# A decoder layer on eight cores: V's first pass on unshifted rows, the second norm by tiles, the residual and the down projection's loads asked for earlier

## The chip, the cores and the metric

One Trainium2 chip, eight cores, one program on all of them. The time is that of the slowest core, in microseconds of device time. Each core has TensorE (PE), VectorE (DVE), ScalarE (ACT), GpSimd (POOL, here only the issuer of the weight loads) and SyncE (SP, the issuer of all other transfers). On-chip memory is one hand-managed region of 128 partitions x 53184 words ("arena"); matmuls write to eight PSUM banks of 512 f32.

## The reference, cut to what matters

One layer, D = 4096, four sequences of 2048 tokens, 16 heads, F = 11008:

```python
mod = silu(c) @ w_ada + b_ada        # shift1, scale1, gate1, shift2, scale2, gate2
h = rms(x, norm1_g) * (1 + scale1) + shift1
u, va, q, k, vb, ga, gb = split(h @ w_in)
y_a = gelu(u) * (W_s @ rms(gelu(va)) + b)       # in chunks of 128 tokens
# per head two softmaxes over keys of 128, causal, with ALiBi
y_b = rms((softmax(q1 k1) - lam * softmax(q2 k2)) @ vb) * (1 - lambda_init)
x = x + gate1 * ((sigmoid(ga) * y_a + sigmoid(gb) * y_b) @ w_out)
h2 = rms(x, norm2_g) * (1 + scale2) + shift2
x = x + gate2 * ((silu(conv(h2 @ up_g)) * conv(h2 @ up_v)) @ w_down)
```

## The kernel before

Two cores share a sequence. The even one (half 0) owns tokens 0 to 1119, the odd one (half 1) the rest; it also computes K and V for its context, tokens 0 to 1023, and 94 tokens of its own first block again. Activations lie transposed, features on partitions. Weights stream as slices of 256 columns (4 MB in f32 in memory, cast to 2 MB on chip) through a ring of three slots, `w_run`. A unit is a slice and the code that consumes it; the slice of unit i is asked for at most two units ahead, once its slot's last reader is done (`w_issue`, L410). The order on each engine is the order in which the program is written out; a small clock (`tick`) only decides where background pieces (`bg_set`) and delayed pieces (`later`) are put into it. DMAs of SP and POOL run in two queues.

Stages, in order:

- **Front** (`mixer`, L585 to L622): 16 units of w_ada for scale1, then 16 for shift1, 64 matmuls of one column each (L340 through `ada_unit`). Beside them the first pass over x: squares on ACT (L492), sums on DVE (L494), and for each tile of tokens a matmul with ones (L498), ln and exp. When the last unit is through, the second pass scales (L506) and shifts (L508) x into h. Half 1 does this for its context; two of four tiles of x stay on chip.
- **Context, half 1 only**: for each head K (norm by L533, L539, L543 to L545, store to kc_s) and V (`cv`, cast at L655, store to vc_s). Its own x is filled in beside it, from rings of eight (`fill`).
- **vA** (L674 on): gelu (L682), squares (L683), store to vA_s, 16 heads.
- **Heads**: K, Q, V, gB, gA, u for each. The attention of the head before runs in the background of K, Q and V: scores L805, exp L811, values L823, and at each block's end a tail of small operations (L834 to L847) that frees the banks of the values.
- The other 64 w_ada units stand between these units, one behind every second in half 1, behind each in half 0; six are held back for the last head's attention.
- **Output projection** (`out_proj`): a block is 32 matmuls (L1019) and a DVE operation with the gate and the residual, which is loaded when the block begins (L1014, L1026); the sum goes to x1_s.
- **Second norm** (`norm2`): one root for each tile (L1067), then all x1 read again, scaled (L1075) and shifted (L1077) into h2.
- **Up projection**: 86 units, convolution on DVE, products kept on chip for the first chunks (19 of 86 in half 1, 15 in half 0), stored to act_s for the others.
- **Down projection** (`down`): when the up projection has ended, w_down pieces of 11 chunks go to a ring of four and act_s is loaded back; for each of 32 output rows 86 chunks are summed.

## Time and profile before

| | |
|---|---|
| time, median of the runs shown | 9345.61 us |
| lowest, highest | 9320.87, 9478.41 us |
| profiled execution | 9307.9 us |
| its span, core 7 (half 1, slowest) | 9306.3 us |
| core 6 (half 0, its neighbour) | 9295.3 us |
| all cores | 9282.5 to 9306.3 us |
| core 7: PE, DVE, ACT busy | 8451.6 (91%), 1803.1 (19%), 1996.5 (21%) us |
| core 7: DMA | 1051.87 MB, 113 GB/s |
| largest group | L340 PE, 41728 matmuls, 6446.9 us |

The page divides the span into 40 slices; on core 7 PE's busy tenths are 1, 1, 6 in the first three, then 9 but for a 6 at the 26th. A matmul's own record overlaps its neighbours; where matmuls follow one another without a gap, the stretch divided by their number is the cost of one. The sizes of the DMA queues count what lands; a weight slice is read as twice that. Even cores run one program and odd cores another, so a change has to be followed on both.

### The profile page before, as it was taken

To read this page: it belongs to the slowest core of one execution; us is meant where nothing else is said; L and a number is where in the kernel's file an instruction comes from. 1 tells how busy PE (TensorE), PEld (TensorE's weight loads), DVE (VectorE), ACT (ScalarE), POOL (GpSimd) and SP (SyncE) were. 2 spreads that over 40 slices of the span, in tenths; PEclk is the share of its full clock that TensorE was granted. 3 is DMA by queue.
4 is the path that set the end of the run, shared out by engine and by line. 5 is a ranking of instruction groups with operands and counts; after the bars stand their busy time and mean duration, and the time that the engine had idled before them with its cause. 6 is when DMAs were issued, how large, how long until landed. Compare 5 with 4: busy or idle time off the path is not lost.

```text
span 9306.3 us, 141632 instructions; the slowest of 8 cores (9282.5 to 9306.3 us)
## 1 busy us (share of the span) xinstructions
PE 8451.6 (91%) x56406; PEld 4878.7 (52%) x56406; DVE 1803.1 (19%) x3402; ACT 1996.5 (21%) x4411; POOL 315.9 (3%) x602
## 2 busy tenths in 40 slices
PE   1169999989999999999999989699999999989999
PEld 1146567865565555555555544344444444444444
DVE  2032220001221112222221121322322222200000
ACT  2042221222333333333333320211111111100000
POOL 0000000000000000000000000000000000001111
PEclk9999999999999999999999989899999999999999
DMA  9977776664545544454433366644444444466666
GB/s 193 174 159 151 154 148 124 123 124 94 107 95 107 109 101 101 100 98 94 81 66 83 69 154 143 163 82 82 93 98 92 91 92 96 86 149 113 113 113 105
DMA packets 298092, 1051.87 MB, mean 113 GB/s; under 512 B 29536, under 2 KB 214624, under 8 KB 253664
## 3 DMA queue, kind: packets, MB, share of 16 engines
q0 software_dynamic: 86112, 807.44, 47.5%
q1 hardware_dynamic: 211328, 235.27, 8.3%
q8 instruction: 466, 7.63, 0.3%
q14 instruction: 186, 1.52, 0.1%
HBM read 1770.85 MB, written 79.14 MB: 199 GB/s over the span
## 4 chain that ended last, share of the span: by engine, by line
PE 71%; DMA 18%; DVE 3%; ACT 3%; issue 2%; another core or an unknown queue 1%; SPq 1%; DVEq 0%; ACTq 0%; POOLq 0%
PE ps L340 54%; PE ps L1204 11%; DMA arena<-x_loc 6%; DMA vA_s<-arena 5%; PE ps L823 4%; DMA arena<-w_ada 2%; PE ps L805 2%; DMA vc_s<-arena 2%; DMA arena<-x_ctx 1%; ACT arena L811 1%; DMA kc_s<-arena 1%; ACT arena L842 1%; DVE arena L837 1%; DVE arena L839 1%
## 5 line engine op out<-in xcount | busy, mean ns | idle before, releaser
L340 PE MATMUL ps<-arena 128*128 128x465 bf16 (+3 forms) x41728 | 6446.9, 308 | 378.9 <-DMA arena<-w_ada 242.2
L340 PEld LDWEIGHTS ps<-arena 128*128 128x128 bf16 x41728 | 3588.0, 98 | 2777.7 <-issue 420.7
L1204 PE MATMUL ps<-arena 128*128 128x464 bf16 x5504 | 1087.1, 360 | 33.1 <-DMA arena<-w_down 17.3
L1204 PEld LDWEIGHTS ps<-arena 128*128 128x128 bf16 x5504 | 533.1, 97 | 587.1 <-issue 45.3
L811 ACT ACTIVATE arena<-ps,arena 128x256 bf16<-128x256 f32 (+1 forms) x1600 | 693.0, 456 | 647.4 <-PE ps L805 638.0
L823 PE MATMUL ps<-arena 128*128 128x257 bf16 (+1 forms) x3200 | 614.4, 276 | 144.4 <-ACT arena L811 92.3
L1129 ACT ACTIVATE arena<-ps 128x465 f32<-128x465 f32 x344 | 192.3, 559 | 1900.5 <-PE ps L340 1900.5
L823 PEld LDWEIGHTS ps<-arena 128*128 128x128 bf16 (+1 forms) x3200 | 258.4, 97 | 406.5 <-issue 292.7
L1019 PE MATMUL ps<-arena 128*128 128x465 bf16 x2048 | 417.9, 368 | 28.4 <-DVE arena L1026 27.6
L805 PE MATMUL ps<-arena 128*128 128x128 bf16 (+1 forms) x3200 | 434.8, 218 | 0.0
L1119 DVE TENSOR_SCALAR arena<-arena 128x928 f32<-128x928 f32 x172 | 131.3, 764 | 1487.7 <-ACT arena L1129 1487.7
L1122 DVE SCALAR_TENSOR_TENSOR arena<-arena 128x928 f32<-128x928 f32 x344 | 407.7, 1185 | 36.3 <-DVE arena L1122 0.5
L916 ACT ACTIVATE arena<-ps 128x465 bf16<-128x465 f32 x192 | 107.5, 560 | 1172.2 <-PE ps L340 1166.4
L805 PEld LDWEIGHTS ps<-arena 128*128 128x128 bf16 x3200 | 296.5, 98 | 82.1 <-issue 31.8
L1019 PEld LDWEIGHTS ps<-arena 128*128 128x128 bf16 x2048 | 202.5, 99 | 243.4 <-issue 48.1
L452 DVE TENSOR_TENSOR arena<-ps,arena 128x2 f32<-128x2 f32 x96 | 15.1, 157 | 1493.6 <-PE ps L340 1493.6
L545 DVE SCALAR_TENSOR_TENSOR arena<-ps,arena 128x512 bf16<-128x512 f32 (+1 forms) x192 | 141.0, 735 | 759.3 <-ACT arena L544 647.5
L1209 DVE SCALAR_TENSOR_TENSOR arena<-ps,arena 128x464 f32<-128x464 f32 x64 | 44.9, 701 | 1070.7 <-PE ps L1204 1070.7
L419 POOL DMA_DIRECT2D arena<-w_in x144 | 76.0, 528 | 4679.7 <-PE ps L340 3818.1
L508 ACT ACTIVATE arena<-arena 128x256 bf16<-128x256 f32 x256 | 114.9, 501 | 407.0 <-DVE arena L506 406.9
L492 ACT ACTIVATE arena<-arena 128x256 f32<-128x256 f32 x256 | 102.4, 413 | 381.5 <-DMA arena<-x_ctx 194.1
L533 ACT ACTIVATE arena<-ps 128x512 bf16<-128x512 f32 (+1 forms) x192 | 111.3, 579 | 297.9 <-PE ps L340 260.3
(74 smaller groups left out, 2303.1 us busy)
## 6 DMA issues: line engine op xcount, KB each, us to landing
arena<-w_in POOLq DMA_DIRECT2D x144, 2048.0 KB, 14.2
arena<-w_ada POOLq DMA_DIRECT2D x96, 2048.0 KB, 24.1
arena<-w_up POOLq DMA_DIRECT2D x86, 2048.0 KB, 13.8
arena<-w_down POOLq DMA_DIRECT2D x224, 352.0 KB, 4.8
arena<-x_loc SPq DMA_DIRECT2D x256, 128.0 KB, 4.1
arena<-w_out POOLq DMA_DIRECT2D x16, 2048.0 KB, 14.1
arena<-x_ctx SPq DMA_DIRECT2D x128, 128.0 KB, 3.8
act_s<-arena SPq DMA_DIRECT2D x67, 232.0 KB, 9.2
```

The lines of the kernel that those rows point to most:

```text
L340: fns = [(lambda e, l=l, rr=rr, i=i: e.matmul(out, lhsT=l, rhs=rr, start=(i == 0), stop=(i == n - 1))) for i, (l, rr) in list(enumerate(pa ...
L508: P.op("act", lambda e: e.activation(out=dst[:, fc, a:a + w], in_=xv, func=AF.Identity, bias=self.modT[:, fc:fc + 1], scale=1.0), reads=[x ...
L533: P.op("act", lambda e: e.activation(out=sqb.v[a][:, 0:w], in_=o, func=AF.Square), reads=[self.Bps[bk]], writes=[sqb.b[a]])
L545: P.op("dve", lambda e: e.scalar_tensor_tensor(out=dst, in0=o, scalar=self.cc(gname), in1=rv, op0=ALU.mult, op1=ALU.mult), reads=[self.Bps ...
L805: P.op("pe", [(lambda e, cm=cm: e.matmul(sv[:, cm * w:(cm + 1) * w], lhsT=KT[:, cm, kb * 128:kb * 128 + m], rhs=QT[:, cm, q0:q0 + w], star ...
L811: P.op("act", lambda e: e.activation(out=pv, in_=sv, func=AF.Exp, bias=self.cc("ali", ai)[0:m, :], scale=128.0 ** -0.5), reads=[self.Bps[s ...
L823: P.op("pe", [(lambda e, cm=cm: e.matmul(self.ps[0:w, (6 + cm) * 512:(6 + cm) * 512 + 257], lhsT=self.pT.v[pt][0:m, cm * w:(cm + 1) * w], ...
L1019: fns = [(lambda e, kc=kc: e.matmul(o, lhsT=wv[:, kc, l * 128:(l + 1) * 128], rhs=self.hy[:, kc, t0:t0 + w], start=(kc == 0), stop=(kc == ...
L1119: P.op("dve", lambda e: e.tensor_scalar(out=dst, in0=src[:, 0:NO], scalar1=cw(0), scalar2=self.cc("convb", ch), op0=ALU.mult, op1=ALU.add) ...
L1122: P.op("dve", lambda e, jj=jj: e.scalar_tensor_tensor(out=dst, in0=src[:, jj:NO + jj], scalar=cw(jj), in1=dst, op0=ALU.mult, op1=ALU.add), ...
L1129: P.op("act", lambda e: e.activation(out=dst[:, z + t0:z + t0 + w], in_=o, func=AF.Copy), reads=[self.Bps[bk]], writes=[Bd], acc=True)
L1204: P.op("pe", [(lambda e, kc=kc: e.matmul(o, lhsT=w6.v[k][:, kc - a, :], rhs=self.hb6[:, kc, t0:t0 + w], start=(kc == 0), stop=(kc == FFC - ...
```

## The change

1. **Scale first, V next, shift beside it.** The 16 scale units run alone, with five slots (two more cut from memory that is free then) and four slices ahead. Beside them a new class `Front` puts x * s1c, neither normed nor shifted, into h for the first tile of 384 tokens. V for tokens 0 to 1119 (half 0) or the context (half 1) is then computed from such rows, each row of the result scaled by its token's root in the copy out of PSUM, and stored to vc_s. Three heads run together tile by tile while the next tile of x is prepared, ten follow with the shift's slices spread between them (two before each of the first five, one before each of the next five, one behind), and the last three run together by tile, while h proper is made from x, read again, tile by tile.
2. **V without the shift's part.** In each head 64 matmuls of one column give shift @ W_v (`v_bias`), spread over partitions by an f32 matmul; (1 - lambda) times it is added in the attention's tail, since softmax rows sum to one. Half 1 subtracts it from its own tokens' V. Half 0 computes no V in the heads: it loads it from vc_s, but still reads V's weight slice for the bias.
3. **Half 1's context K** alone beside the fill of its own x, now with rings of 24 and 16 and two weight slots.
4. The 58 w_ada units that are not held back are spread over vA and the heads.
5. **Output projection**: slots alternate, eight banks, a ring of up to six for the residual, asked for five blocks ahead; the sum is written in place. The last two slices are taken together, tile by tile.
6. **Second norm by tiles**: a tile's root and its 32 steps run in the background of the next tile's blocks, the last one's in the first two slices of the up projection, which are taken together too.
7. **Up and down**: more chunks stay on chip (34 in half 1, 20 in half 0). The down projection's rings wait only for what lay where they lie; eight (six) sums are built at once, over the chunks on chip first, then in the order in which memory comes free.

The diff, cut:

```diff
+class Front:
+    def raw(self, ti, fc):
+        P.op("dve", lambda e: e.tensor_scalar_mul(out=self.dst[:, fc, a:a + w], in0=xv, scalar1=X.s1c[:, fc:fc + 1]), ...)
+        ...
+        if fc == self.FC - 1:
+            X.later(3000, lambda: self.roots(ti), [("rs", ti)])
...
+        def scale_unit(p, u):
+            def consume(wv, wb):
+                u[1](wv, wb)
+                for fc in range(2 * p, 2 * p + 2):
+                    fr.raw(0, fc)
+            return (u[0], consume, 5, None, 4)
...
+        def v_raw(h, wv, wb, span):
+            def epi(b, m, bk, o):
+                ti = b * 128 // 384
+                self.force(("rs", ti))
+                k = self.take(st)
+                dv = st.v[k][0:m, 0:256]
+                P.op("dve", lambda e: e.tensor_scalar_mul(out=dv, in0=o, scalar1=fr.rsT[0:m, b:b + 1]), ...)
+                P.op("sp", lambda e: e.dma_start(out=T["vc_s"][h][0:m, b, :], in_=dv), ...)
+            self.gemm_t(wv, wb, hx, B0, tiles0, n0, epi, span)
+
+        def v_first(held):
+            for ti, (a, w) in enumerate(tiles0):
+                self.bg_drain()
+                if ti + 1 < NT:
+                    self.bg_set(fr.gen(fr.raw, ti + 1), 0.85 * ng * -(-w // 128) * blk)
+                for h, (wv, wb) in enumerate(held):
+                    v_raw(h, wv, wb, (a, a + w))
...
+        for i, u in enumerate(mid):
+            n = -(-len(left) // (len(mid) - i + 1))
+            units += left[:n] + [u]
+            del left[:n]
...
+        def v_bias(h, wv, wb):
+            for l in range(2):
+                self.mm(bk, o[:, l:l + 1], [(wv[:, kc, l * 128:(l + 1) * 128], self.shb[:, kc:kc + 1]) for kc in range(FC)], ...)
+            ...
+            def spread():
+                P.op("pe", lambda e: e.matmul(o2, lhsT=self.ones_f, rhs=dg.rearrange("p a b -> p (a b)"), start=True, stop=True), ...)
+                P.op("dve", lambda e: e.tensor_scalar_mul(out=self.bl.v[h % 2], in0=o2, scalar1=self.omlam), ...)
...
-                P.op("dve", lambda e: e.tensor_scalar_mul(out=ov, in0=O[:, 0, 0:256], scalar1=rl[:, 0:1]), ...)
+                P.op("dve", lambda e: e.scalar_tensor_tensor(out=ov, in0=O[:, 0, 0:256], scalar=rl[:, 0:1], in1=self.bl.v[h % 2][0:w, :], op0=ALU.mult, op1=ALU.add), ...)
...
             def cv(wv, wb, h=h, k=k):
+                v_bias(h, wv, wb)
                 ...
-                self.gemm_t(wv, wb, hloc, Bh, ftiles, LT, epi)
+                if r.half == 1:
+                    self.gemm_t(wv, wb, hloc, Bh, ftiles, LT, epi)
...
+            n = order.index((cc, ti))
+            while len(got) < min(len(order), n + xx["x"].n - 1):
+                got.append(load_x(*order[len(got)]))
...
+                self.force("root")
+                span = 4 * FC * (w / 2.4 + 2.5)
+                self.later(0.6 * span if ti else 2500, lambda ti=ti, span=span: self.norm2(ti, span), ["root"])
...
+        self.pre = [ch for ch in range(FFC) if at(ch)[1] <= hi - tail_words or (at(ch)[0] >= h2end and at(ch)[1] <= self.WR0)]
...
-        w6 = Ring(P, A, "w6", 4, [128, KG, 128], BF16, dma=True, over=dead)
+        w6 = Ring(P, A, "w6", 4, [128, KG, 128], BF16, dma=True)
+        for k in range(4):
+            w6.b[k].over = dead(A.top - (4 - k) * KG * 64, A.top - (3 - k) * KG * 64)
...
+        per = min(FC, max(1, 8 // len(r.otiles)))
+        plan = [(list(range(per)), [(a, b) for a, b, _ in runs])]
+        plan += [([cc], [(a, min(FFC, a + KG)) for a in range(0, FFC, KG)]) for cc in range(per, FC)]
```

## Rows read from the trace of the kernel before

**Rows 1.** stretches of core 7: busy us (xcount) by engine, then clock, DMA share, GB/s

```profile
0.00:560.00 560.00, 85.25 (x2137) 68.60 (x2138) 115.02 (x311) 116.20 (x277) 18.81 (x39) 0.97 0.95 181
...
560.00:1560.00 1000.00, 945.31 (x7183) 630.46 (x7182) 197.91 (x455) 228.06 (x448) 25.33 (x48) 0.97 0.72 146
...
6030.00:8180.00 2150.00, 2149.84 (x10903) 1061.59 (x10901) 628.43 (x595) 263.73 (x426) 43.81 (x83) 1.00 0.45 89
```

**Rows 2.** stretches of core 6, same columns

```profile
0.00:570.00 570.00, 82.35 (x2184) 73.95 (x2184) 109.39 (x244) 106.96 (x203) 18.81 (x39) 0.97 0.95 185
...
570.00:1150.00 580.00, 544.63 (x5545) 479.59 (x5546) 2.84 (x17) 129.21 (x436) 16.88 (x32) 0.97 0.67 126
```

**Rows 3.** waits of PE, core 7, 0 to 560 us: total us, times, longest

```profile
PE ps L340 <- DMA arena<-w_ada: 242.2, 23, 12.9
...
PE ps L498 <- DVE arena L494: 160.0, 4, 56.5
```

**Rows 4.** DMA queues of core 7, 50 to 75 us: packets, MB, share of 16 engines

```profile
q0 software_dynamic: 274, 3.97, 96.0%
q1 hardware_dynamic: 274, 0.26, 4.6%
```

**Rows 5.** DMA queues of core 7, 425 to 450 us

```profile
q0 software_dynamic: 289, 4.21, 100.6%
```

**Rows 6.** DMA queues of core 7, 525 to 550 us

```profile
q1 hardware_dynamic: 4896, 4.46, 70.0%
```

**Rows 7.** DMA queues of core 7, 2010 to 2020 us

```profile
q1 hardware_dynamic: 96, 0.05, 2.3%
```

**Rows 8.** DMA queues of core 7, 2025 to 2035 us

```profile
q1 hardware_dynamic: 1008, 0.46, 15.6%
```

**Rows 9.** line L682, core 6, 500 to 1300 us: what ended ACT's idle time

```profile
  DMA vA_s<-arena: 204.4, 50
```

**Rows 10.** timeline of core 7: start, us, engine, line, names, count

```profile
1989.73 56.67 PE L340 MATMUL ps<-arena 128*128 128x256 bf16 x515
```

**Rows 11.** groups by form, core 7, 560 to 1500 us: busy us, mean ns, idle before

```profile
L539 PE MATMUL ps<-arena 128*128 128x512 bf16 x59 | 23.5, 398 | 44.3 <-ACT arena L533 44.3
...
L498 PE MATMUL ps<-arena 128*128 128x256 f32 x8 | 3.2, 486 | 10.4 <-DVE arena L494 10.4
```

**Rows 12.** timeline of core 7 behind the second norm's start

```profile
5969.25 6.22 DVE L1075 SCALAR_TENSOR_TENSOR arena<-arena 128x465 f32<-128x465 f32 x10 [0.48 <-DMA arena<-x_s]
```

**Rows 13.** waits of PE, core 7, 5880 to 6100 us

```profile
PE ps L340 <- ACT arena L1077: 64.2, 2, 49.3
```

**Rows 14.** waits of PE, core 7, 5500 to 5880 us

```profile
PE ps L1019 <- DVE arena L1026: 23.7, 7, 4.0
```

**Rows 15.** waits of PE, core 7, 8080 to 8300 us

```profile
PE ps L1204 <- DMA arena<-w_down: 17.3, 1, 17.3
PE ps L1204 <- DMA arena<-act_s: 15.8, 5, 6.6
```

**Rows 16.** waits of PE, core 6, whole span

```profile
PE ps L340 <- ACT arena L1077: 71.4, 3, 44.6
...
PE ps L1019 <- DVE arena L1026: 52.4, 13, 7.3
...
PE ps L340 <- ACT arena L682: 48.3, 12, 13.5
...
PE ps L1204 <- DMA arena<-act_s: 23.0, 7, 8.4
...
PE ps L1204 <- DMA arena<-w_down: 18.2, 1, 18.2
```

**Rows 17.** groups by form, core 7, 2110 to 5300 us

```profile
L340 PE MATMUL ps<-arena 128*128 128x1 bf16 x2176 | 60.8, 163 | 0.0
...
L837 DVE TENSOR_SCALAR arena<-ps,arena 128x256 f32<-128x256 f32 x105 | 50.8, 484 | 11.6 <-DVE arena L834 0.5
...
L839 DVE SCALAR_TENSOR_TENSOR arena<-ps,arena 128x256 f32<-128x256 f32 x105 | 50.8, 484 | 11.9 <-DVE arena L838 1.2
```

More of the change, by code:

```diff
@@ L471, in fill, with load @@
         Brs = [Buf(f"rs{i}", over) for i in range(len(tiles))]
[L472 to L475 removed]
+        def load(xin, ti, fc):
             a, w = tiles[ti]
[L477 to L482 removed]
             k = xin.next()
@@ L608, in mixer @@
[L608 to L628 removed]
+            n0, hx, src = LT, hloc, T["x_loc"]
@@ new lines, in v_first, with v_last @@
+        def v_first(held):
[5 more added lines that the diff above has]
+                    v_raw(h, wv, wb, (a, a + w))
+        def v_last(held):
+            P.op("dve", lambda e: e.tensor_copy(out=self.shb, in_=self.modT[:, 0:FC]), reads=[self.Bmod[0]], writes=[self.Bshb])
+            fr.again()
+            for ti, (a, w) in enumerate(tiles0):
+                for i, (wv, wb) in enumerate(held):
+                    v_raw(H - ng + i, wv, wb, (a, a + w))
+                self.bg_set(fr.gen(fr.final, ti), 0.8 * ng * -(-w // 128) * blk)
@@ new lines, in k_first @@
+            def k_first(held):
+                for ti, t in enumerate(tiles0):
+                    if ti == NT - 1:
+                        self.bg_drain()
+                    for h, (wv, wb) in enumerate(held):
+                        k_ctx(h, wv, wb, [t])
+                if H > nk:
+                    span = (H - nk) * 2 * FC * sum(w / 2.4 + 2.5 for _, w in ctt)
+                    self.bg_set(fill_gen(), span * 0.9 / len(fills))
+            nk = min(2, ng)
+            units += self.together([(W(OK, h), None, 2, None, 2) for h in range(nk)], k_first)
@@ new lines, in mixer @@
+            for h in range(nk, H):
+                units.append((W(OK, h), lambda wv, wb, h=h: k_ctx(h, wv, wb, ctt), 2, None, 2))
+        def va_bufs():
+            self.force("norm")
+            A = A1 if r.half == 0 else Arena(self.arena, self.R1, self.WR0)
+            ov = [] if r.half == 0 else over1
+            self.vst = Ring(P, A, "vst", 12, [128, 256], BF16, dma=True, over=ov)
+            self.junk = A.alloc([128, 256], BF16); self.Bjunk = Buf("junk", ov)
+            self.ssq = A.alloc([128, r.nlb, H], F32); self.Bssq = Buf("ssq", ov)
@@ new lines, in va_first @@
+        def va_first(held):
+            for ti, (a, w) in enumerate(ftiles):
+                if ti == len(ftiles) - 1:
+                    self.bg_drain()
+                if ti == 0:
+                    va_bufs()
+                for h, (wv, wb) in enumerate(held):
+                    va(h, wv, wb, (a, a + w))
+        h0 = 0
+        if r.half == 0:
+            units += self.together([(W(OVA, h), None, 3, None, 2) for h in range(ng)], va_first)
+            h0 = ng
+        for h in range(h0, H):
@@ L1153, in unit, with slots_of, take @@
-            return (T["w_up"][ch], consume, 2 if ch == 0 else 3, None, 1 if ch == 1 else 2)
-        return [unit(ch) for ch in range(FFC)]
+                dsts = take()
+                for ti in range(len(r.qtiles)):
+                    tile(wv, wb, dsts, ti)
+                rest(ch, dsts)
+            return (T["w_up"][ch], consume, slots_of(ch), None, 0 if ch == 2 else 2)
+        def slots_of(ch):
+            return (1,) if ch == 0 else (0,) if ch == 1 else 3
+        def take():
+            out = []
+            for n in ("g", "v"):
+                k = bb[n].next()
+                out.append((bb[n].v[k], bb[n].b[k]))
+            return out
@@ new lines, in first_two @@
+        def first_two(held):
+            for ti in range(len(r.qtiles)):
+                while ti not in self.normed:
+                    if self.bg is None:
+                        self.force("root")
+                    else:
+                        self.bg_step()
+                if ti == len(r.qtiles) - 1:
+                    self.bg_drain()
+                    self.wr.b[2].over = list(self.xr_bufs)
+                    self.tab("silu_and_others")
+                if ti == 0:
+                    bufs()
+                    ds = [take() for _ in held]
+                for (wv, wb), d in zip(held, ds):
+                    tile(wv, wb, d, ti)
+            for ch, d in enumerate(ds):
+                rest(ch, d)
@@ L1156, in down @@
+        units = [unit(ch) for ch in range(FFC)]
+        return self.together(units[:2], first_two) + units[2:]
     def down(self):
```

588 lines of the change are left out of this document (367 added, 221 removed).

## The prediction, made before the changed kernel ran

> **What bounds the kernel now.** I read the stretches of both kinds of core first, then PE's waits stretch by stretch, then the DMA queues in short windows. Even cores hold a sequence's first 1120 tokens, odd cores the rest; the slowest is core 7, and core 6 is its even neighbour. Four stretches are not PE-bound. (1) The front. For 560 us core 7's PE is busy 85 us at a DMA share of 0.95, core 6 the same [rows 1, 2]: 32 slices of w_ada come in while PE waits 242 us for slices and 160 us in the root matmul L498, which stands in PE's order ahead of the next slice's matmuls and needs a whole tile of x [rows 3]. (2) Between L1019 and the up projection PE waits 64 us for h2 on core 7, 71 us on core 6 [rows 13, 16]. (3) In the output projection the residual's late load holds L1026 and through it PE, 24 and 52 us [rows 14, 16]. (4) The down projection starts 33 and 41 us late, for its weights and the reloaded activations [rows 15, 16]. Elsewhere PE is full: 2149.8 of 2150 us in the up projection [rows 1].
>
> What fixes the front's price is how the two DMA queues share. Alone, the slice queue lands 4.21 MB (two slices, read as twice the bytes) in 25 us, 12.4 us a slice [rows 5]. With x loads queued beside it slices still get 3.97 MB, 13.2 us each, and the x queue gets 0.26 MB in 25 us [rows 4]; with no slices about, it gets 4.46 MB [rows 6]. Stores with 512 B packets do 0.05 MB in 10 us beside slices, 0.46 MB without [rows 7, 8]. So the slow queue moves only when the slice queue has nothing to load. That is already felt: on core 6 ACT idles 204 us for vA_s stores, and PE waits 48 us for L682 [rows 9, 16]. The Trainium skill (DMA: Bandwidth & Descriptors, Queues, rings and completion order) says that each DMA engine takes turns between its queues packet by packet, which fits this: a slice's packets are far larger. Its Specifications give about 358 GB/s of HBM to a core, by which a slice would take an estimated 11.7 us and 21 of them 31 us less than by the row; the row decides.
>
> **The change, part by part, core 7.** The sum goes against its profiled span of 9306 us (9308 us with what lies around it; the three runs shown have median 9346, lowest 9321).
>
> *Scale slices.* Sixteen scale units with five slots and four ahead; x tile 0 (384 tokens, 32 x 0.197 = 6.3 MB) is asked for beside them. PE's first V matmul needs all of tile 0, and the slices don't wait: 16 scale, 3 V and 2 shift slices fill the slots, 21 x 13.2 = 277 us. The x queue has moved meanwhile 0.26 MB per 25 us times 1.5 (its rows are 1.5 kB here, not 1 kB), 4.3 MB; the other 2.0 MB take 11 us at 0.178 MB/us. V starts at 3 + 277 + 11 = 291 us.
>
> *First three heads of V.* A block of 128 tokens is 32 matmuls of 110 ns, since 515 took 56.67 us [rows 10]; so 8 blocks x 3 heads = 84.5 us. All five slots are full, so x has its queue: tile 1 at 0.178 MB/us is 35 us against 32 us of PE, 4 us late; 8 us more for a restart at the lower clock, an estimate. 388 us.
>
> *Ten middle heads with the shift's slices.* Work of PE is 28.2 us a head and 1.8 us a slice (64 x 28 ns [rows 17]). DMA: two shift slices and one V slice are 39.6 us, so the first five are bound by DMA. Each head also stores 8 x 64 kB = 0.52 MB. During 39.6 us of slices 0.20 MB of it go; the rest wait till PE, out of store buffers (four, and four banks), holds up the slots, and then go at 0.046 MB/us: 7 us. A cycle is 46.6 us. What waits there is DVE's scaling of a block, for a store buffer; behind it in DVE's order stand the next blocks and L452 of the shift slices, and for them PE, once its four banks are full. The last five have one shift slice: 26.4 us of slices, 0.13 MB drained, 8.5 us for the rest: 34.9 against 30 us of PE. Together 28 + 4 x 46.6 + 5 x 34.9 = 389 us, end 777. This is the choice that matters: without the stores' term it would be 28 + 4 x 39.6 + 5 x 30 = 336.
>
> *Last three heads, final pass over x.* 84.5 + 2 us; x comes again (16.8 MB, 94 us at 0.178) with 24 stores (34 us), against 125 us until K needs its last tile; 10 us late. End 874.
>
> *K for the context.* Before, 945 us were busy over V, K, 15 ada units (27 us) and L539 (59 in 23.5 us [rows 11]): K is 945 - 451 - 27 - 25 = 442, with its norms 467 us. The fill of the second half's own x (33.5 MB) stood beside 889 us of GEMM and stands now beside 14 x 27.6 = 387 us. Rings are 24 and 16 deep instead of 8. From both sides: nothing, if they cover it; 57 us by the rival below. I take 20. End 1361, where the stretch ended at 1560 [rows 1]: 199 us less. The 16 ada units that stood there go into the heads: +16 x 1.8 = 29 us. Net -170.
>
> *Bias in the heads.* V is now kept without the shift's part, and (1 - lambda) times that part is added in the attention's tail. 16 x 64 matmuls of one column at 28 ns = 1.8 us a head, and one f32 matmul of 256 columns, by L498 (3.2 us for 4 tiles) 0.8 us: 16 x 2.6 = +42 us. The tail's L837 becomes a two-input form from PSUM; L839 is that form and takes the same 484 ns [rows 17]: nothing. The subtraction that replaces a cast of V is taken at nothing too: it hides under the next block's 3.5 us of PE, and if that cover went, each 0.1 us on 128 blocks would be 13 us.
>
> *Second norm by tiles.* A block of the up projection is 32 x 197 ns = 6.3 us (10903 in 2149.8 [rows 1]), so a tile over two slices is 25 us. DVE needs 32 x 0.62 = 20 us for a tile [rows 12] and some 5 us for the blocks' own work, after 6 us of root and loads: PE waits about 6 us for the first tile, 16 for the second (its root comes at 0.6 of the tile before), 2 + 2 for the two up slices that must wait for the output projection's slots, and 1.3 for the table. 28 of 64 us stay; with less time at the low clock -41.
>
> *Residual early.* Ring of six, asked for five ahead, eight banks: the 23.7 us go [rows 14]. What is late next is the x1_s store of that ring, with 30 us to land. -24.
>
> *Down.* 34 chunks stay on chip instead of 19, come first, and give 34 x 8 x 0.197 = 53 us of cover while 52 chunks (12 MB) load; weights load into the slot that is free early. Three runs of one chunk starve the four-deep weight ring, some 2 us each. -27 of 33 [rows 15].
>
> Sum: -170 + 42 - 41 - 24 - 27 = -220: 9086 us.
>
> **Core 6.** Same start. 95 + 12 us to 398; a ninth block makes cycles of 48.1 and 36.4: 31.7 + 192 + 182, to 804; last three 107, to 911; vA 580 - 6 x 1.8 = 569, to 1480, against 1150: +330. V's GEMM leaves the heads: 16 x 9 x 32 x 110 ns = -507. Six ada units more +11, bias +42, norm -45, residual -50, down -27. Sum -246: 9049. It reads V's weights twice, 16 slices more, covered: a head has 7 to 9 slices, about 110 us, in some 180. So core 7 sets the time. Runs lie 13 to 38 us above the profiled one; I take 14 over the sum: 9100.
>
> **Rivals.**
> *A. Stores don't bind.* The slice queue pauses often enough by itself. For it: vA_s lands in 1.5 us when slices pause (the queue moved 0.46 MB in 10 us [rows 8]). Against it: ACT's 204 us [rows 9]. It saves 53, with the 20 and 10 us of the fills 83: 9017. Chance 0.22.
> *B. The fill starves K.* 33.5 MB at 0.178 MB/us are 188 us, 8.4 MB of K stores at twice the 512 B rate 91 us, 14 slices 185: 464 us for 387, so 57 more than my 20: 9157. For it: the x queue stands still beside slices [rows 4]. Against it: deeper rings keep that queue full. Its sign in the trace is ACT L533 late and PE in L539. Chance 0.20.
> *C. Slower: the slice queue never pauses.* With five slots, if PE never held them up, the middle heads' 0.52 MB would go at 0.005 MB/us, 104 us each: 1040 instead of 389 us, 9751. It makes the kernel slower than before from 61 us a middle head on. Against it: at most four slices are ahead, 53 us. Chance 0.04.
> *D. As forecast.* 0.54.
>
> **How the numbers follow.** The time is that of D. Its own range is 9050 to 9150. The range reaches below A, whose norm and down terms could also be 25 better, and above B with the norm's 41 us not gained: 8990 to 9205. Faster by over 2% means under 9159, about what a measurement can tell from no change: D nearly whole, A, a small part of B: 0.72. Within 2%: 0.24. Slower: 0.04.
>
> **What would show it.** The first 256-column matmuls at 291 us (right if 270 to 310); K of the context starting at 850 to 900; vA at 1330 to 1390 on core 7; in the middle heads PE idle 10 to 18 us a cycle, DVE there waiting for vc_s stores; L1077 waits under 35 us, L1026 near nothing, first down waits under 10. It is wrong if V starts after 330, if PE waits over 60 us in L539 and L498 during K, or if the attention's waits (L823) grow by more than 30 us.

## The result: 1.1% faster, where 2.6% was forecast

| | before | after |
|---|---|---|
| median of the runs | 9334.6 us | 9225.7 us |
| lowest, highest | 9320.87, 9478.41 us | 9215.03, 9242.6 us |
| ratio, 95% interval | | 0.989 (0.9863 to 0.9916) |
| profiled execution | 9307.9 us | 9242.6 us, core 1 slowest |
| odd cores, median of the last instruction's end | 9295 us | 9217 us |
| even cores, the same | 9288 us | 9061 us |

The forecast was 9100 us with a range of 8990 to 9205. The time lies above it, and within 2% of before. In some executions the cores of one die run at a lower granted clock and the time is some per cent longer, so the times compared below are those of executions, and in `a_nobias` of cores (4 to 7), without that. The even cores gained 227 us, where 246 were forecast; the odd ones, which set the time, 78 of 220.

The stages by the odd cores' medians (us from the span's start; the last column is read for core 7 from the prediction). V's first pass goes here from the first to the last copy of V out of PSUM (L732; L655 before), an output projection from its first matmul:

| | before | after | forecast |
|---|---|---|---|
| V's first pass | 574 to 1555, K beside it | 295 to 908 | 291 to 874 |
| K of the context, to vA's start | to 1572 | 547 us | 487 us |
| vA's start to the attention's end | 3899 us | 4003 us | +71 |
| output projection | 439 us | 411 us | -24 |
| its end to the up projection's end | 2255 us | 2233 us | -41 |
| down projection and end | 1125 us | 1110 us | -27 |

Stretches of the slowest core, 1, after, cut at these stages: busy us (xcount) of PE, its loads, DVE, ACT and POOL, then clock, DMA share, GB/s. The answers of before are [rows 1].

```profile
0.00:300.00 300.00, 49.08 (x1153) 43.81 (x1154) 42.35 (x123) 26.43 (x51) 11.43 (x25) 0.98 0.99 183
300.00:910.00 610.00, 501.77 (x5020) 429.46 (x5018) 125.24 (x300) 55.06 (x113) 15.30 (x29) 0.89 0.70 140
910.00:1460.00 550.00, 482.38 (x2283) 225.94 (x2282) 171.53 (x367) 246.48 (x514) 8.97 (x17) 0.93 0.68 154
...
5875.00:5915.00 40.00, 11.01 (x48) 4.96 (x47) 13.93 (x22) 12.19 (x19) 0.53 (x1) 0.65 0.82 207
5915.00:8107.00 2192.00, 2171.82 (x10903) 1068.69 (x10902) 649.23 (x627) 286.38 (x460) 46.49 (x88) 0.99 0.45 91
```

Two stretches that should be full are not: in the second PE idles 108 of 610 us at a granted clock of 0.89, in the third 68 of 550 at 0.93. The DMA share in both is about 0.7, while it was 0.99 in the first: over the stage the DMA engines were not full either, though the prediction had put V's stall down to slices that keep them busy. Core 1 was the slowest in V: its stage took 631 us, the other odd cores' 603 to 617.

Waits of PE, core 1, whole span: total us, times, longest. L440 is the matmul helper (L340 before), L567 the addition that ends an ada unit (L452 before), L732 V's scaling out of PSUM, L1299 the shift into h2 (L1077 before), L1042 the attention's tail (L839 before).

```profile
PE ps L440 <- DVE arena L567: 124.1, 10, 25.0
PE ps L440 <- DMA arena<-w_ada: 92.5, 8, 12.5
PE ps L440 <- DVE arena L732: 92.0, 12, 15.6
PE ps L1025 <- ACT arena L1013: 87.3, 190, 1.4
PE ps L648 <- ACT arena L642: 62.2, 8, 25.7
PE ps L440 <- ACT arena L1299: 49.2, 2, 29.0
PE ps L1025 <- DVE arena L1042: 48.1, 51, 2.0
...
PE ps L648 <- DVE arena L327: 19.1, 1, 19.1
PE ps L1498 <- DMA arena<-w_down: 18.8, 13, 4.0
```

The wait for the residual of [rows 14, 16] is gone, the root's 160 us of [rows 3] too (L567 and the slices stand there now). The wait for L1299, 64.2 before [rows 13], is shorter by 15 us only, and the 18.8 for w_down stand for the 33.1 for w_down and act_s before [rows 15]. L732 is new. Who holds it up is seen on DVE and SP in the same stretch, 300 to 910 us:

```profile
DVE arena L732 <- DMA vc_s<-arena: 271.7, 39, 18.4
DVE arena L732 <- PE ps L440: 192.8, 74, 6.5
...
SPq L187 <- DMA vc_s<-arena: 348.8, 65, 30.1
```

DVE waits for stores to vc_s, as forecast. The last line is what the prediction missed: SP itself, which only issues transfers, waits 349 us for stores to vc_s to land. The code says why. All blocks of a head write one dependency record (`writes=[Bvs[h]]`), so a store is ordered behind the landing of the head's previous one, though they write different rows. Of a head's stores, 64 kB each, one is then under way at a time; behind the waiting SP stand the later stores and the loads of x.

### The profile page after: what moved, and what is told of

Read it like the earlier page. It is cut to its first block, busy times and chain, and to the rows that moved or that the text cites. A ratio compares the mean times of both kernels' runs of the same rounds, so it can differ in the third digit from the quotient of the medians.

```text
span 9241.0 us, 144391 instructions; the slowest of 8 cores (9052.7 to 9241.0 us)
## 1 busy us (share of the span) xinstructions
PE 8550.7 (93%) x57608; PEld 4960.5 (54%) x57608; DVE 1847.9 (20%) x3521; ACT 1981.6 (21%) x4363; POOL 326.5 (4%) x622
## 4 chain that ended last, share of the span: by engine, by line
PE 79%; DMA 11%; ACT 3%; DVE 2%; issue 2%; another core or an unknown queue 2%; SPq 0%; DVEq 0%; ACTq 0%; POOL 0%; POOLq 0%
PE ps L440 57%; PE ps L1498 12%; DMA vA_s<-arena 4%; PE ps L1025 4%; PE ps L1233 4%; DMA vc_s<-arena 3%; PE ps L1007 2%; DMA arena<-x_ctx 1%; ACT arena L1013 1%; DVE arena L1039 1%; DVE arena L1042 1%; ACT arena L1045 1%; DMA kc_s<-arena 1%; ACT arena L652 0%
## 5 line engine op out<-in xcount | busy, mean ns | idle before, releaser
L440 PE MATMUL ps<-arena 128*128 128x465 bf16 (+3 forms) x42880 | 6540.8, 306 | 411.8 <-DVE arena L567 124.1
L440 PEld LDWEIGHTS ps<-arena 128*128 128x128 bf16 x42880 | 3658.6, 98 | 2830.8 <-issue 455.8
L1498 PE MATMUL ps<-arena 128*128 128x464 bf16 x5504 | 1089.1, 360 | 18.8 <-DMA arena<-w_down 18.8
L1498 PEld LDWEIGHTS ps<-arena 128*128 128x128 bf16 x5504 | 533.0, 97 | 574.7 <-issue 35.4
L1025 PE MATMUL ps<-arena 128*128 128x257 bf16 (+1 forms) x3200 | 625.5, 280 | 153.5 <-ACT arena L1013 87.3
L1025 PEld LDWEIGHTS ps<-arena 128*128 128x128 bf16 (+1 forms) x3200 | 261.6, 98 | 412.8 <-issue 296.8
L1007 PEld LDWEIGHTS ps<-arena 128*128 128x128 bf16 x3200 | 300.4, 100 | 87.5 <-issue 33.0
L1233 PEld LDWEIGHTS ps<-arena 128*128 128x128 bf16 x2048 | 200.1, 98 | 207.8 <-issue 5.7
L567 DVE TENSOR_TENSOR arena<-ps,arena 128x2 f32<-128x2 f32 x96 | 14.9, 156 | 1483.5 <-PE ps L440 1483.5
L654 DVE SCALAR_TENSOR_TENSOR arena<-ps,arena 128x512 bf16<-128x512 f32 (+3 forms) x196 | 142.0, 724 | 777.3 <-ACT arena L653 639.0
L1485 POOL DMA_DIRECT2D arena<-w_down x276 | 145.7, 528 | 1021.2 <-PE ps L1498 977.3
L652 ACT ACTIVATE arena<-ps,arena 128x512 f32<-128x512 f32 (+3 forms) x196 | 130.6, 666 | 201.0 <-PE ps L648 200.9
L329 ACT ACTIVATE arena<-arena 128x384 bf16<-128x384 f32 (+1 forms) x96 | 49.3, 575 | 545.0 <-DVE arena L327 544.8
```

The lines of the kernel that those rows point to most:

```text
L440: fns = [(lambda e, l=l, rr=rr, i=i: e.matmul(out, lhsT=l, rhs=rr, start=(i == 0), stop=(i == n - 1))) for i, (l, rr) in list(enumerate(pa ...
L652: P.op("act", lambda e: e.activation(out=rv, in_=xo, func=AF.Ln, bias=self.cc("eps"), scale=1.0 / 128), reads=[self.Bps[xb], self.Bcst], w ...
L654: P.op("dve", lambda e: e.scalar_tensor_tensor(out=dst, in0=o, scalar=self.cc(gname), in1=rv, op0=ALU.mult, op1=ALU.mult), reads=[self.Bps ...
L1007: P.op("pe", [(lambda e, cm=cm: e.matmul(sv[:, cm * w:(cm + 1) * w], lhsT=KT[:, cm, kb * 128:kb * 128 + m], rhs=QT[:, cm, q0:q0 + w], star ...
L1025: P.op("pe", [(lambda e, cm=cm: e.matmul(self.ps[0:w, (6 + cm) * 512:(6 + cm) * 512 + 257], lhsT=self.pT.v[pt][0:m, cm * w:(cm + 1) * w], ...
L1233: fns = [(lambda e, kc=kc: e.matmul(o, lhsT=wv[:, kc, l * 128:(l + 1) * 128], rhs=self.hy[:, kc, t0:t0 + w], start=(kc == 0), stop=(kc == ...
```

## Experiments

Times of stages are medians over the four odd cores of the profiled execution, unless told otherwise. All kernels but the two named `b_` change the changed kernel. Only `a_unchain_quarter` and `b_quarter` have an interval; what is said of the others rests on the profiled execution, in the main, and on the agreement of its cores.

**1. Smaller pieces for the slices.** The edit, in the changed kernel (`a_quarter`) and in the one before (`b_quarter`):

```diff
-            P.op("pool", lambda e, dst=dst, src=src: e.dma_start(out=dst.rearrange("p a b -> p (a b)"), in_=src), ...)
+            fl, n = dst.rearrange("p a b -> p (a b)"), self.c.FC * 256 // 4
+            P.op("pool", [lambda e, ...: e.dma_start(out=fl[:, x * n:(x + 1) * n], in_=src[:, x * n:(x + 1) * n]) for x in range(4)], ...)
```

> The changed kernel with one edit: each weight slice is asked for in four transfers of a quarter of the columns instead of one, so that what the slice queue lands in one piece is 4 kB instead of 16 kB. Theory T (the two queues take turns piece by piece, so the slow queue's share beside slices goes with the ratio of piece sizes): beside slices the x queue moves some 50 to 60 GB/s instead of 15, and 512-byte stores 15 to 20 GB/s instead of 4 to 5; in the middle heads of V on odd cores DVE L732's 264 us of waiting for vc_s stores falls below 90; V's pass ends at 850 to 880 us instead of 905 to 926, K takes 490 to 510 us instead of 545; the slowest core ends 80 to 130 us earlier, about 9110 us. Rival R (the front is bound by the bytes or by the memory, and stores wait because all transfers do): L732 still waits over 200 us, the stages end within 15 us of where they did, the time stays within 0.3% of 9225. Rival S (more transfers on POOL cost more than they give): slices land later than 15 us median and the time goes above 9250.

> The kernel before with the same edit (each slice in four transfers of a quarter). Theory T: the x loads of the first pass no longer stand still beside slices, so L498's 160 us of PE waiting in the front falls below 80 and ACT's 204 us of waiting for vA_s stores on core 6 below 60; the front ends 20 to 50 us earlier, the time falls by 30 to 80 us. Rival R (bytes bind): the front is full of slices anyway, so 32 slices and the x take as long as before: time within 0.3% of before, whatever the waits are called.

The queues of core 1 in the changed kernel and then in `a_quarter`, 50 to 75 us: packets, MB, share of 16 engines.

```profile
q0 software_dynamic: 262, 3.77, 89.2%
q1 hardware_dynamic: 262, 0.35, 6.8%
```

```profile
q0 software_dynamic: 937, 3.41, 83.0%
q1 hardware_dynamic: 939, 1.28, 21.0%
```

In each pair the two queues moved the same number of packets, 262 and 262, 937 and 939: while both have work they take turns, one packet each. A slice's packet is 14.4 kB in the first (3.77 MB / 262) and 3.6 kB in the second, so the slow queue went from 0.35 to 1.28 MB, and both together from 4.1 to 4.7 MB. The Trainium skill (DMA: Bandwidth & Descriptors, SWDGE vs HWDGE vs iDMA) would have a packet be at most 4096 B preferably, as the point at which an engine changes queues; the trace shows what the larger one costs beside a second queue.

V's first copy out of PSUM then came 28 us earlier (268 against 295). But V's stage stayed as long, 616 against 613 us, and SP's wait grew:

```profile
SPq L187 <- DMA vc_s<-arena: 401.8, 83, 17.7
```

20 us of the earlier start were lost again at once: PE now waited 20.0 us for the root of x's second tile (L309 behind DVE's L284). In the ten middle heads alone, from the first shift slice's matmul to the last one's, the stretch fell from 426 to 392 us. K took 529 instead of 547 us. The odd cores ended at 9145, 72 us earlier.

The kernel before gained too: 9248.9 us, ratio 0.990 (0.9871 to 0.9929), odd cores 9295 to 9202, even ones 9288 to 9238. ACT's wait for vA_s on core 6 fell from the 204 us of [rows 9] to 65.5. The other half of the expectation failed: PE's wait in the root matmul fell only from 160 [rows 3] to 141.2 us. So the queue's share is real, but in V it is not what binds alone.

**2. No stores in V's first pass** (`a_nostore`). It leaves out all vc_s stores behind each head's first block; the heads load rows of vA_s in their place, in the same number and size.

```diff
-                P.op("sp", lambda e: e.dma_start(out=T["vc_s"][h][0:m, b, :], in_=dv), ...)
+                if b == 0:
+                    P.op("sp", lambda e: e.dma_start(out=T["vc_s"][h][0:m, b, :], in_=dv), ...)
```

> The changed kernel with V's first-pass stores to vc_s left out for all blocks but the first of a head; the heads load their V from vA_s instead, of the same size, so the output is not the reference's. Forecast D's term (stores bind the middle heads): without them V's pass on odd cores ends 50 to 90 us earlier than 905 to 926, at 830 to 860 us, and DVE L732 waits for PE alone. Rival A (stores don't bind, the slices do): it ends within 15 us of the same time, with PE waiting for w_ada and w_in slices for what L732 took before.

V's stage fell from 613 to 520 us, 93 less, and the middle heads from 426 to 334; the odd cores ended at 9116. (DVE still waited 69.1 us for the stores that were left.) The forecast's V stage was 583 us, 53 of it for stores (28 + 389 against 28 + 336), 530 without. For the middle heads it had 389 and 336. So all else in it was right to 10 us, and the stores' term was 40 too small.

**3. Stores not chained** (`a_unchain`), alone and with the slices in four pieces (`a_unchain_quarter`). One record for each block of vc_s, kc_s and vA_s; who loads a head waits for all of its records.

```diff
-        Bvs = [Buf(f"vcs{h}") for h in range(H)]
+        Bvs = [[Buf(f"vcs{h}_{b}") for b in range(9)] for h in range(H)]
...
-  ... reads=[st.b[k]], writes=[Bvs[h]], dsem=st.s[k])
+  ... reads=[st.b[k]], writes=[Bvs[h][b]], dsem=st.s[k])
```

> The changed kernel with one edit: each store of a block to vc_s, kc_s and vA_s gets its own dependency record, so that SP no longer waits for the landing of the head's store before it (SPq L187 waited 330 us for vc_s landings in the middle heads; a store took 10 to 14 us to land beside slices). Nothing else moves. Theory C (the chain: one store in flight at a time is what bound the middle heads, not the share of the queue): on odd cores V's pass ends 50 to 80 us earlier than 908, near the 820 of the kernel without stores, DVE's wait for vc_s falls below 100 us, the slowest core ends near 9140. Rival T (the share: beside slices 512-byte pieces move at 5 GB/s however many stores are in flight; only the stretches without slices get faster): V's pass ends within 20 us of 908, DVE still waits over 180 us, the slowest core ends within 30 us of 9215.

> The changed kernel with both edits: unchained stores, and slices in four transfers of a quarter. If the share of the queues counts (T) and the chain kept the quarter slices alone from showing it (V's pass stayed at 616 us with them, each store still took 8.7 us to land), both together bring V's pass on odd cores to under 560 us, its end to 820 to 840 with the start at 267, and the slowest core to 9070 to 9100. If the chain alone counts (C), the two add up: V's pass as long as in a_unchain, 28 us earlier, the slowest core some 70 us below a_unchain. If neither (bytes bind), V's pass stays above 600 us.

| V's stage; the middle heads; end of the odd cores | one piece | four pieces |
|---|---|---|
| chained | 613; 426; 9217 us | 616; 392; 9145 us |
| not chained | 599; 410; 9158 us | 569; 347; 9087 us |

What the stores' queue got beside slices shows both limits. The queue lines of core 1, 440 to 465 us, a stretch in which slices were loading in all four: changed kernel, `a_unchain`, `a_quarter`, `a_unchain_quarter`. The slice queue had 286, 279, 1029 and 1072 packets.

```profile
q1 hardware_dynamic: 222, 0.11, 2.0%
```

```profile
q1 hardware_dynamic: 279, 0.13, 2.5%
```

```profile
q1 hardware_dynamic: 417, 0.19, 3.8%
```

```profile
q1 hardware_dynamic: 957, 0.43, 8.7%
```

DVE's waits, 300 to 900 us, in `a_unchain` and then in `a_unchain_quarter` (where L732 is L733), and SP's in `a_unchain`:

```profile
DVE arena L732 <- DMA vc_s<-arena: 248.2, 25, 15.0
```

```profile
DVE arena L733 <- PE ps L440: 364.3, 117, 13.0
```

```profile
SPq L187 <- DVE arena L732: 456.5, 98, 17.2
```

Without the chain SP no longer waits for its stores, and they take a turn for each packet of a slice (279 and 279). But the slices' packets are large, so the stores get 0.13 instead of 0.11 MB, and DVE still waits 248 us for a buffer. With smaller pieces but the chain, the stores use 417 of 1029 turns. Only with both do they get 0.43 MB, and DVE waits for PE alone. In the middle heads the pieces alone saved 34 us, the records alone 16 (407 to 416 us on the four cores, against 418 to 444), and both together 80 of the 92 that the stores cost. `a_unchain` alone met neither of its theories: the stage is that of the queue's share (14 us less), but the odd cores ended 59 us earlier, of it 14 in K and 18 in the attention. Over the whole kernel the two remedies simply add up: 59 and 72 us alone, 130 together. The attention's part doesn't: either alone took 18 to 20 us off it, and so did both.

V's stage stays 49 us above the 520 without stores, and above the 560 that was expected. On core 1 PE's waits account for 30 of them: 21.2 us for the root of the second tile where `a_nostore` had 1.1, and 32.9 us for w_in slices, which now share with the stores, where it had 23.2.

`a_unchain_quarter` took 9093.3 us, ratio 0.9758 (0.9714 to 0.9803) to the kernel before, which does not settle whether it is 2% faster. It is the fastest version with an interval, its median 132 us below that of the changed kernel. It has odd cores at 9087 and even ones at 8970.

**4. Pieces of 2 kB** (`a_uq8`: as before, 8 in place of 4), and **both remedies on the kernel before** (`b_unchain_quarter`).

> The changed kernel with both remedies, and each weight slice as eight transfers of 2 kB a row instead of four of 4 kB. Theory 1 (the share of the slow queue goes by the size of the pieces, and it still binds): V's first pass shrinks further, 569 to about 555 us, K's stretch from 528 to about 515 and the wait for h2 from 50 to about 40 us, in all 9087 to about 9050. Theory 2 (at 4 kB the slow queue is no longer what binds; slices themselves get slower, or nothing changes): V 565 to 575, K 525 to 530, total within 10 us of 9087, or above it if the first V start (263 us) comes later.

> The kernel before, with both remedies that brought the changed kernel from 9217 to 9087 us on the odd cores: each weight slice as four transfers of 4 kB a row, and one dependency record for each block that is stored, so that a store no longer waits for the one before it to land. Theory 1 (the stall of slow-queue stores was made by the change, since it put V's stores beside the densest slices): here PE is full behind the first 560 us, so the second remedy adds little to the 9202 us that quarter slices alone gave: 9185 to 9205, and the change is then worth about 100 us or more once both kernels have the remedies. Theory 2 (the remedies help any schedule alike): about 9090 to 9130, and the change itself is worth next to nothing. SP's wait for vc_s (255 us with quarter slices alone) should be gone under both.

`a_uq8`: V 564 us, K 535, odd cores 9094, against 569, 528 and 9087: with 2 kB there is nothing more to have. `b_unchain_quarter`: odd cores 9176, slowest core of the profiled execution 9184.4 us; SP's wait for vc_s, 225 us before on core 7, is not in core 1's list. This lies just below theory 1's 9185 to 9205, and far from theory 2. But theory 1's reason was too narrow: the remedies took 119 us off the old schedule (9295 to 9176) and 130 off the new one (9217 to 9087). The path of the small transfers was nearly as expensive before, only spread over other stages: 76 us up to vA's start, 20 in the attention, 22 in the output projection. By the odd cores the change itself is worth 78 us without the remedies and 89 with them.

**5. The fill beside K.** `a_nofill` leaves out all loads of the odd cores' own x behind the first ring of each pass, and `a_uq_nofill` does the same with both remedies; the work on DVE and ACT is kept, on stale rows.

```diff
-            P.op("sp", lambda e: e.dma_start(out=xv, in_=src[fc * 128:(fc + 1) * 128, t0 + a:t0 + a + w]), ...)
+            if xin.i <= xin.n:
+                P.op("sp", lambda e: e.dma_start(out=xv, in_=src[fc * 128:(fc + 1) * 128, t0 + a:t0 + a + w]), ...)
```

> The changed kernel where the odd cores' fill of their own x beside the context's K loads only the first 24 and 16 chunks and then works on what lies in the rings; all ACT, DVE and PE work of the fill stays, 28 MB of loads go; the output is not the reference's. Theory B (x loads starve K's stage): K takes 485 to 500 us instead of 545 and the waits of L648 for L642 fall from 36 to under 10 us. Rival N (ACT's and DVE's order in K's stage, not the loads): K still takes 535 to 550 us with the same waits.

> The changed kernel with both remedies; the odd cores' fill of their own x leaves out all loads behind the first ring of each pass (so wrong rows go into h, the work on DVE and ACT is kept). It splits K's stretch (odd cores, 528 us with the remedies, 487 in the forecast). Theory 1 (what is left is not the loads: the first K blocks behind the final pass over x, the norm's waits for ACT, the lower clock behind these gaps): 518 to 528 us. Theory 2 (the loads still bind): under 505 us. Even cores must not move (8970).

K's stage: 547 to 523 us, and with the remedies 528 to 506. The loads cost 24 and 22 us either way, near the 20 taken for them. 523 meets neither theory of the first run, and 506 falls between the two theories of the second run: of the 41 us above the forecast that the remedies left, the loads explain about half. The rest is in PE's waits there, 820 to 1345 us, core 1:

```profile
PE ps L650 <- DVE arena L327: 12.9, 1, 12.9
PE ps L650 <- ACT arena L644: 12.9, 4, 9.6
PE ps L440 <- DMA arena<-w_in: 9.0, 1, 9.0
PE ps L608 <- DVE arena L604: 5.6, 4, 2.9
```

506 less these 40.4 is 466, and the forecast's K with norms was 467: the work was about right, the waits were not in it.

**6. No bias but the first head's** (`a_nobias`): `v_bias` runs for head 0 only, its result is used in all.

> The changed kernel with the shift's part of V worked out for head 0 alone and used for all heads (64 one-column matmuls, the small DVE work and the f32 matmul of 15 heads are gone; the output is not the reference's). The heads' stretch (end of vA to end of attention) is 3538 us on odd cores against 3440 before. Forecast (bias 42 us, moved w_ada units 29): it falls by 35 to 45 us to about 3500, and what stays over 3440 beyond the 29 is another cost. Rival (the bias costs far more than its own matmuls, because its DVE steps and its f32 matmul stand in the attention's way): it falls by 60 to 70 us, to 3470.

vA's end to the attention's end took 3487 us against 3538. The bias of fifteen heads costs 51 us, between the two theories, 3.4 a head where 2.6 was forecast. Its own matmuls are the 2.6: 64 of 28 ns and two records of L933, 379 ns each. PE's idle time was the same without it (186 against 185 us on cores 5 and 7); its busy time fell by 51, 38 of it these matmuls. The rest goes with the granted clock of the stretch, 0.986 without the bias and 0.979 with it; no run separates the two.

**7. The second tile's root earlier** (`a_uq_root`, with both remedies).

```diff
-                self.later(0.6 * span if ti else 2500, ...)
+                self.later(0.15 * span if ti else 2500, ...)
```

> The changed kernel with both remedies; the second tile's root of the second norm is put in at 0.15 of the span of the tile before instead of 0.6. PE waits there twice, 29.5 and 20.4 us, and DVE waits 18.3 us for x1_s in the same window. Theory 1 (the second wait is the root's due time: its 32 steps of 0.62 to 0.7 us start only at the root): the second wait falls from 20 us to under 8, total -12 to -18 us, 9069 to 9075 on odd cores, even cores as much or more. Theory 2 (the second tile's steps wait for x1_s loads behind the up slices in the queues): the second wait stays above 15 us and the total within 5 us. The first wait, 29.5 us, should stay under both.

PE, core 1, 5740 to 5900 us, in `a_unchain_quarter` and then in `a_uq_root`:

```profile
PE ps L440 <- ACT arena L1300: 49.9, 2, 29.5
```

```profile
PE ps L440 <- ACT arena L1300: 37.2, 2, 31.2
```

The second wait fell from 20.4 to 6.0 us, as theory 1 has it, and the first stayed. The odd cores ended 9 us earlier (9078), a little short of the 12 to 18 expected; the even ones, with three tiles, 13 later (8983), which neither theory had. As the even cores are not the slowest it would pay, but one execution of 9084.2 us can't be told from the other's 9090.6 to 9094.9.

## Point by point

The miss on the odd cores is 142 us. By stage: 82 in the front, 33 in vA and the heads, 19 in the second norm, 12 in the down projection, less 4 in the residual.

**Scale slices, V's start: the number right, in part by luck.** The x queue's share was near what was read: 0.35 MB in 25 us, where 0.39 had been taken (0.26 times 1.5 [rows 4]). But tile 0 was complete, and the first 256-column matmul began, at 267 us and not at 291. After two blocks PE stood still until 292 for the tile's root: ACT's L313 comes in ACT's order behind squares of the next tile, which waited for their x (12.2 and 11.4 us on core 1). So x came 24 us sooner than forecast, and a wait that the forecast did not have took them back. PE's wait there, core 1:

```profile
PE ps L440 <- ACT arena L313: 14.3, 1, 14.3
```

**The middle heads' stores: the kind of stall right, the term 53 us, measured 93.** The failing step is the cycle, "during 39.6 us of slices 0.20 MB of it go; the rest ... 0.046 MB/us", 46.6 us in the first five heads and 34.9 in the last five: 389 us, where 426 were measured. Two things in it were off: its rates, a little, and its pauses.

The rates were read in a stretch [rows 7, 8] in which the stores were chained already, as SP's own waits say (core 7 before, 2010 to 2040 us):

```profile
SPq L187 <- DMA vA_s<-arena: 26.2, 9, 14.8
```

In the middle heads they were somewhat lower still: 0.11 MB in 25 us beside slices, which is 0.0044 MB/us for the 0.005 taken, and 64 kB in 1.6 us, 0.041 for 0.046, without. By these two rates the forecast's own sum gives an estimated 402 us instead of 389.

The larger part is the pauses. The slice queue stood still for 70 to 96 us between 363 and 805 us, worked out from the slices' issues and landings on the odd cores; in `a_nostore` it did so for under 3 us (cores 1 and 3), in `a_unchain_quarter` not at all (cores 1 and 5). The forecast's cycles hold 70 us of pause too, but it took 18 of them to be there without stores as well, since PE was to bind the last five heads. They weren't: all of the pause is lost. And a pause lasts as long as it takes PE to free a slot, not as long as the stores need: on core 1 two of them were 29 and 27 us, a whole head of PE (28.2 us). They ended when slices were asked for at 585.4 and 676.9 us, 0.5 us behind the last V matmul of a head (584.9 and 676.4). The stores landed at once in the pauses:

```profile
vc_s<-arena SPq DMA_DIRECT2D x123, 64.0 KB, 1.6
```

(issues of core 1, 300 to 910 us: number, size, median us to landing; beside slices one took 10 to 24 us as a rule, and 30.6 at most). That the shared record has a part in it is shown by `a_unchain` and `a_unchain_quarter`. Its sign was in the trace of before, core 7, 560 to 1560 us:

```profile
SPq L187 <- DMA vc_s<-arena: 225.2, 96, 14.5
```

The prediction counted what SP's queue moves but never read what SP itself waited for. The first three and the last three heads were shorter than forecast, so that V ended 34 us late.

**K of the context: 487, measured 547.** The failing step is the equation of the stage with its work, 467, and one term of 20 for the fill. That term was right (24). Left out, or nearly so, were, on core 1 (910 to 1460 us), 19.1 us before the first ones matmul of K, since the last V block ended but the final pass over x (L327) still waited for x_ctx; 36.5 us of L648 behind ACT's squares L642, which stand in ACT's order behind the fill's own squares and shifts; 8.7 for a slice with two slots; 5.6 for roots; in all 70 of the 80 us above 467. The last 10 are put down to the clock of 0.93, which no run shows. Part of the 36.5 is the loads' 24 in another guise: ACT itself waited 47.6 us for x_loc there (L616 38.4, L600 9.2). The prediction had written 10 us for the final pass, at V's end, and nothing for the other three, though L539 already waited 44 us for L533 [rows 11] before.

**vA and heads: +71, measured +104.** Core by core the stretch grew by 97 us (median); the other 7 come from the table's differences of medians. The bias took 54 (16 times 3.4) instead of 42, the moved ada units 29. Of the other 14, 10 are idle time of PE, 172 to 182 us in the heads. PE waited 48.1 us for L1042, where L839 had 37.0, and 12.2 for L1017, where L815 had 6.5, but 5.7 less for the exp and 4.7 less in L648. The longer waits are not the bias's: without it they stayed (46.3 and 13.8 on core 5 of `a_nobias`). Nor are they the tail's new form (core 1, 1920 to 5458 us; L837 and L839 are L1039 and L1042 now), which takes the 484 ns forecast:

```profile
L1039 DVE SCALAR_TENSOR_TENSOR arena<-ps,arena 128x256 f32<-128x256 f32 x111 | 53.7, 484 | 11.5
L1042 DVE SCALAR_TENSOR_TENSOR arena<-ps,arena 128x256 f32<-128x256 f32 x111 | 53.7, 484 | 12.5 <-DVE arena L1041 1.2
```

What makes these waits longer, and the last 4 us, stay open. The subtraction in place of V's cast was taken at nothing: it took 419 ns against 421.

**Residual: right** (28 against 24).

**Second norm: -41, measured -22.** It forecast 6 us for the first tile and 16 for the second; they were 29.0 and 20.2. DVE, core 1, behind the last block of the first tile (L1297 is the scaling, L1075 before):

```profile
5875.33 0.70 DVE L1297 SCALAR_TENSOR_TENSOR arena<-arena 128x465 f32<-128x465 f32 x1
...
5885.32 0.70 DVE L1297 SCALAR_TENSOR_TENSOR arena<-arena 128x465 f32<-128x465 f32 x1 [9.29 <-DMA arena<-x_s]
...
5900.41 1.36 DVE L1297 SCALAR_TENSOR_TENSOR arena<-arena 128x465 f32<-128x465 f32 x2 [11.07 <-DMA arena<-x_s]
...
5906.37 4.38 DVE L1297 SCALAR_TENSOR_TENSOR arena<-arena 128x465 f32<-128x465 f32 x7
```

The failing step is "DVE needs 32 x 0.62 = 20 us for a tile": in [rows 12] the x1_s loads had the queues to themselves, since the last up slice had landed at 5969.0 us, and here two were issued in their midst (5870.6 and 5883.2 us, landed at 5886.5 and 5901.1). It is the rule of the front, which the prediction had itself written down, not applied to the other place where the change puts loads beside slices. That the slices hold the loads up is read from these times; no run moved the slices away. Four pieces did not cure it (51.2 us in `a_quarter`, where DVE waited for x1_s in shorter waits but 27.1 us in all, against 24.9), nor did the other remedy (47.7) or both (49.9).

**Down: -27, measured -15.** The late weights and reloads of [rows 15] went, and 18.8 us of waits for w_down came, 13 times and 4.0 at most. A term for this had been named, that the pieces of one chunk starve the ring of four, and set at 2 us for each of three runs of one chunk: 6 in all. That the 13 waits lie in these runs is inferred from the code.

**Even cores: 9049, measured 9061.** Within 12 us, but by two errors that cancel: V ended at 938 instead of 911, and vA took 525 us instead of 569, which stays unexplained.

**The rivals.** A (stores don't bind) is refuted: they cost 93 us. B (the fill starves K, 57 us more) has its sign, PE waiting for ACT's L642 and for L327, but the loads cost 24 us and not B's 77, 4 more than the forecast took: most of the other waits stayed without them. Whoever had read only the sign would have held it shown. C did not come about. What decided was a sum of five terms, each too small, and mostly for the same want: a stage was priced by its work and by the full rate of its queue, and what waits for what within it was left at little or nothing. The range reached up to B's price with the norm's 41 us not gained, on the thought that the other terms would scatter about their values; all five erred to one side.

**The signs.** Right: DVE waiting for vc_s, PE idle about 11 us a head in the middle heads (106 in ten on core 1), the residual, and the attention's waits (L1025, +11 us, under 30). Just outside: the first 256-column matmul, at 267 instead of 270 to 310. K's first matmul came at 884 to 910 us, mostly inside 850 to 900, but the first norm, for which PE then waited, only at 913 to 939. Wrong, and so showing the failing steps: vA at 1455 instead of 1330 to 1390, L1299 49 instead of under 35, the down's first waits 19 instead of under 10. One sign of being wrong was met: in K, PE waited 61 to 67 us in L648 and L606 (L539 and L498 before) on the four odd cores, and the line was 60.

## To carry to other kernels

Read what the issuing queue itself waits for. If an issuer waits for its own transfers to land, the stores are chained, and a rate read there is that of the chain; a dependency record shared by disjoint rows is enough to make it. When a stall holds up the slots of the bulk queue, price the pause by what it takes to free a slot, not by what the small transfers need. If a bulk queue runs beside one of small pieces, cut the bulk into pieces of some kB, and expect little of it where the small transfers go one at a time. When work is moved beside weight slices, apply the measured sharing rule in every stage to which the change moves loads, and give each handover between stages a price of its own.

## What the runs showed of the hardware

Two DMA queues that both had work took turns of one packet: 262 and 262, 937 and 939 packets in 25 us. With packets of 14.4 kB against 1.3 kB the small queue had 0.35 of 4.1 MB; with 3.6 kB against 1.4 kB it had 1.28 of 4.7 MB. The smaller pieces did not lower the sum, and pieces of 2 kB brought no more. A queue whose transfers were ordered one behind the other left turns unused: 222 packets to 286, and 279 to 279 without the order; 417 to 1029, and 957 to 1072 without it. In the changed kernel a 64 kB store landed in 1.6 us in the median and took up to 30.6 us beside slices.
